# Stick-breaking attention on one core: splitting one k-tile's products in two pieces of columns at eight places

## The reference

```python
h, gate_res = ada_modulate(x, c, norm_g, ada_w, ada_b)
gq, gk, gv, glr, sq, sk, sv, gate = _split(h @ in_w, ODD_SIZES)
...
yd = stick_breaking(hd(sq, SB_HEADS, SB_HEAD_DIM), hd(sk, SB_HEADS, SB_HEAD_DIM),
                    hd(sv, SB_HEADS, SB_HEAD_DIM)).reshape(B_, S, SB_WIDTH)
y = jnp.concatenate([yc, yd], axis=-1) * jax.nn.silu(gate)
return x + gate_res * (y @ out_w)
...
z = jnp.einsum('bthd,bshd->bhts', q[:, q0:q1], k[:, :q1]).astype(jnp.float32) * scale
log_1m = jnp.where(strict, jax.nn.log_sigmoid(-z), 0.0)
after = lax.cumsum(log_1m, axis=3, reverse=True) - log_1m
w = jnp.where(strict, jnp.exp(log_beta + after), 0.0)
outs.append(jnp.einsum('bhts,bshd->bthd', w.astype(v.dtype), v[:, :q1]))
```

## Time and profile before

| what | value |
|---|---|
| time, median of 3 runs | 812.6 us (812.37 to 813.02) |
| profiled execution, its own time | 812.26 us |
| span of that execution, first to last instruction | 810.3 us |
| mean granted TensorE clock | 0.998 of full speed |
| TensorE matmuls | 795.8 us busy (98%), 6984 instructions |
| TensorE weight loads | 784.7 us busy (97%), 6984 instructions |
| VectorE, ScalarE | 641.0 us (79%), 499.2 us (62%) |
| part that the change touches | from 687.06 us to 756.79 us of the span |

### The profile page before, as it was taken

The page is one execution under the profiler, slowest core; times in us unless marked ns, Lnnn a source line. Parts: engine busy times, 40 slices in busy tenths (PEclk is TensorE's granted clock), DMA queues, the critical chain, the costliest instruction groups (busy, mean ns, idle before and its releaser), DMA issues.

```text
span 810.3 us, 17222 instructions
## 1 busy us (share of the span) xinstructions
PE 795.8 (98%) x6984; PEld 784.7 (97%) x6984; DVE 641.0 (79%) x1032; ACT 499.2 (62%) x899; POOL 110.1 (14%) x133
## 2 busy tenths in 40 slices
PE   6999999999999999999999999999999999999996
PEld 6999999999999999999999999999999999999996
DVE  7788599977987879787998899887997568566673
ACT  6576666756667464656676853554686467566652
POOL 0022265401040000000230300001203130000001
PEclk9999999999999999999999999999999999999999
DMA  9934544566567989898777667675665446554441
GB/s 335 392 96 140 179 132 129 154 200 214 193 211 232 366 298 332 310 326 328 254 255 223 219 186 234 227 249 176 207 179 163 138 126 195 180 152 153 148 128 53
DMA packets 47021, 170.41 MB, mean 210 GB/s; under 512 B 5216, under 2 KB 5472, under 8 KB 46688
## 3 DMA queue, kind: packets, MB, share of 16 engines
q1 hardware_dynamic: 46224, 165.31, 61.8%
q10 hardware_dynamic: 720, 4.01, 1.2%
HBM read 168.26 MB, written 1.05 MB: 209 GB/s over the span
## 4 chain that ended last, share of the span: by engine, by line
PE 96%; DVE 1%; ACT 1%; DMA 1%; POOL 1%; issue 0%; SPq 0%; DVEq 0%; POOLq 0%; ACTq 0%
PE bank L196 95%; DMA raw<-in_ws 1%; POOL sq L235 1%; PE bank L199 0%; DVE wl L235 0%; SPq L193 0%; ACT wh L205 0%; ACT sq L202 0%; ACT B1h L202 0%; DVE gd L235 0%; DVE h L223 0%; DVE h L235 0%; DVEq L337 0%; POOLq L337 0%; DVE vt L235 0%
## 5 line engine op out<-in xcount | busy, mean ns | idle before, releaser
L235 DVE TENSOR_TENSOR wl<-raw,wh 128x1024 fp32r<-128x1024 f32 (+1 forms) x260 | 326.2, 1266 | 21.1 <-ACT wh L205 19.9
L205 ACT CAST wh<-raw 128x1024 fp32r<-128x1024 f32 (+1 forms) x260 | 268.9, 1046 | 102.3 <-DMA raw<-in_ws 51.0
L196 PE MATMUL bank<-XAh,wl 128*128 128x256 f32 (+1 forms) x896 | 253.9, 283 | 0.0
L196 PE MATMUL bank<-XAl,wh 128*128 128x256 f32 (+1 forms) x896 | 248.5, 277 | 0.0
L196 PE MATMUL bank<-XAh,wh 128*128 128x256 f32 (+1 forms) x896 | 248.4, 277 | 0.0
L196 PEld LDWEIGHTS bank<-XAh,wl 128*128 128x128 f32 x896 | 168.4, 188 | 2.2 <-issue 0.7
L196 PEld LDWEIGHTS bank<-XAh,wh 128*128 128x128 f32 x896 | 168.5, 188 | 0.1
L196 PEld LDWEIGHTS bank<-XAl,wh 128*128 128x128 f32 x896 | 168.4, 188 | 0.0
L196 PE MATMUL bank<-B1h,wl 128*128 128x256 f32 (+1 forms) x464 | 129.3, 279 | 0.0
L196 PE MATMUL bank<-B1l,wh 128*128 128x256 f32 (+1 forms) x464 | 128.6, 277 | 0.0
L196 PE MATMUL bank<-B1h,wh 128*128 128x256 f32 (+1 forms) x464 | 128.6, 277 | 0.0
(11 more groups left out here) (280 smaller groups left out, 1205.3 us busy)
## 6 DMA issues: line engine op xcount, KB each, us to landing
raw<-in_ws SPq DMA_DIRECT2D x306, 512.0 KB, 4.5
bias<-in_bias ACTq DMA_DIRECT2D x1, 1664.0 KB, 11.8
hK<-in_xk SPq DMA_DIRECT2D x4, 272.0 KB, 5.0
h<-in_xt ACTq DMA_DIRECT2D x1, 1088.0 KB, 7.2
out<-gd SPq DMA_DIRECT2D x4, 256.0 KB, 2.6
raw<-in_ws SPq DMA_DIRECT2D x2, 256.0 KB, 3.7
C<-in_cst SPq DMA_DIRECT2D x1, 512.0 KB, 8.0
crow<-in_crow ACTq DMA_DIRECT2D x1, 512.0 KB, 5.9
```

Of the source, the lines that this page charges most:

```text
L196: return self.real.matmul(*a, **k)
L205: return self.real.copy(*a, **k)
L235: return self.real.tensor_tensor(*a, **k)
```

## The change

In the first unit of each of the eight labels in the table `SPLIT`, one k-tile (the second, k = 1) of the first result tile has its three products made in two pieces of columns. The first piece has the number of columns in the table, 128 or 192, and the second has the rest of the 256. Where tokens move (`sq1`, `sq2`, `sq3`, `oo0`), the new function `in_two` does it, after 6 matmuls of the unit. Where weights move (`sv0` to `sv3`), `three_wide` gets the table's width as its step, after 3 matmuls. Both keep the order of the three products and issue the two pieces of a product one after the other, with the same stationary operand. Everything else stays: data, buffers, semaphores and order.

```diff
+SPLIT = {"sv0": 128, "sq1": 128, "sv1": 192, "sq2": 128, "sv2": 128, "sq3": 192, "sv3": 192, "oo0": 128}
...
                     for c in range(0, width, step):
-                        m = e.matmul(dst[:, c:c + step], a[i], b[j][:, c:c + step], start=first and n == 0 and c == 0,
-                                     stop=last and n == 2 and c + step == width)
+                        z = slice(c, min(c + step, width))
+                        m = e.matmul(dst[:, z], a[i], b[j][:, z], start=first and n == 0 and c == 0,
+                                     stop=last and n == 2 and c + step >= width)
+                return m
+
+            def in_two(dst, a, b, c):
+
+                for i, j in ((1, 0), (0, 0), (0, 1)):
+                    for n in (slice(0, c), slice(c, 256)):
+                        m = e.matmul(dst[:, n], a[i], b[j][:, n], start=False, stop=False)
                 return m
...
+                            if label in SPLIT and (q, k, b, t) == (0, 1, 0, 0):
+                                m = in_two(tile(label, t), (hi[:, k, s], lo[:, k, s]),
+                                           (cols(X[0][:, xk + k, :]), cols(X[1][:, xk + k, :])), SPLIT[label])
+                                continue
...
-                                               512 if label == "vn" and col and q == 6 else 256)
+                                               512 if label == "vn" and col and q == 6 else
+                                               SPLIT[label] if label in SPLIT and (q, k, b) == (0, 1, 0) else 256)
```

## The result

The changed kernel takes 814.82 us (median of 10 runs) against 812.9 us (10 runs) of the kernel before: ratio 1.0025, 95% interval 1.0017 to 1.0033, or +1.92 us. The forecast was 814.45, or +1.85 us.

The account below looks back on a forecast made before the run. TensorE's matmul stream was taken to bound the kernel. Pieces add 2.65 us, the quicker pace behind them gives back 0.80 us: +1.85 us, forecast 814.45 us, range 813.3 to 815.5 us.

Parts of the forecast that it names:

- What bounds the kernel: From 685.98 us TensorE's unbroken 110.26 us chain piece covers all places; changes there go to the end one to one.
- The price of a piece: At the eight places, each piece costs its load, 0.112 us; +0.33 us a place, +2.65 us in all.
- What comes back: Matmuls behind the cuts return from 0.1179 to 0.1135 us each; at most 180 matmuls, -0.80 us.
- I take nearly all: Choice, between 0 and -0.80 us, of how much the quick pace behind the cuts gives back; -0.80 entered the sum.
- 192 with 64 costs what 128 with 128 does: At the cut places, the load sets the price of any piece shorter than 256 columns, whichever way 256 is divided.
- The exception: In `sq1` the scores ran at 695.55, yet the next unit still took 2.91 us; a break is no sure cure.
- the cure: The pieces end the slow pace behind them, giving back up to 0.80 us; missing at half the places or more: 0.22.
- When the dull pace begins: From `sv0` on, the slower pace was said to begin with the matmul at which the moving side changes.
- dull pace: Matmuls of 256 columns start 0.1179 us apart instead of 0.1135, with no other engine waited for.
- the count of ten units: Both units of `sv0` and `sq1`, first units of the other six labels: each 0.09 us too long, 0.9 us in all.

Follow-up runs that it names:

- e3: The changed kernel with `sv1`, `sq3` and `sv3` cut in steps of 64 columns instead of 192 (twelve pieces in `sv1` and `sv3`); 815.62 us.
- e11: The changed kernel with all places cut 128 with 128 and each piece using only 64 of its 128 stationary columns, leaving its result incomplete; 813.21 us.
- e12: The changed kernel with two products cut 128 with 128 and the third 192 with 64 at all eight places; 814.68 us, a single run.
- e9: The changed kernel with each product cut into 64 and then 192 columns at all eight places; 814.47 us.
- e10: The kernel before with one cut only: the first product of the second k-tile in `sq1` in two pieces of 128; 812.46 us.
- e4: The changed kernel with all cuts at 128, each in the second unit of its label instead of the first; 814.85 us.
- e6: The kernel before without cuts; side groups before a change of side, and the scores in `sq1`, moved behind the next unit's first k-tile; 812.27 us.
- e7: As e6, plus one product in `sv0` cut in two pieces; 811.89 us.
- e2: The changed kernel with all eight places cut at 192 with 64 columns; 814.76 us.
- e5: The changed kernel with all places cut at 128, but only the first of the three products in two pieces; 812.89 us.

## Why the prediction was right

**What bounds the kernel** held: the change went to the end one to one, through TensorE's stream. The chain's piece on TensorE stayed unbroken through all eight places, and no other engine came into it there.

**The price of a piece** was the main term, and right: 0.69 us expected for six pieces, 0.68 measured, so +0.325 a place where +0.33 stood. Single places agree: the first matmul of `sq1` comes 0.16 us later behind `sv0` (0.15 expected), and the first unit of `sq2` takes 3.19 us (3.17). The reading that it is the load is shown from both sides: by e3 (pieces half as wide, twice as many, twice the price) and by e11 (stationary operand and load halved, 0.06 instead of 0.11 us). Where the price shows differs from the forecast: the six starts and the first whole one lie within 0.62 us, a little under the 0.64 to 0.71 expected, since the first piece takes only its columns (0.06 us) and the first whole matmul waits for its load instead. The trace agrees with the 0.107 us that the Trainium skill (TensorE: Matmul & The Clock Gate, section "LDWEIGHTS (loading the stationary operand)") gives for 128 columns; the measured distance in a run of short pieces is 0.11. It does not agree with the 0.081 us of that page's "Back-to-back issue gap", which would have given 812.9 us.

**What comes back** was over-sized. "I take nearly all" was 180 matmuls and 0.80 us; it was 129 matmuls and 0.57 us, because behind the three cuts of 192 with 64 the pace stayed dull. The step that failed is the half of the sentence "192 with 64 costs what 128 with 128 does" that I drew without saying it: the price is the same, the effect isn't. The last piece was 64 columns, and e12 and e9 show that at these places this is what matters.

**The exception** that made me doubt the cure, `sq1` behind a dull `sv0`, is not general: it concerns the scores as a break, not a cut of 128 with 128 (e10), and it goes away once `sv0` is quick (e4, e6 with e7). But it is not tied to `sv0` either: in e11 the scores fail in `sq2`, `sq3` and `oo0` as well.

**When the dull pace begins** was read too narrowly. In the last attention it does begin at the change of the moving side. Elsewhere it also begins without one. Timeline of the kernel before from 176 to 184 us, with tokens moving in both units:

```profile
176.48 0.28 PE L196 MATMUL bank<-B0h,wl 128*128 128x256 f32 x1
...
178.88 0.59 PE L196 MATMUL bank<-sq,C 128*128 128x256 f32 x2
179.31 1.03 PE L196 MATMUL bank<-AT,iN 128*128 128x256 f32 x4
...
180.96 0.28 PE L196 MATMUL bank<-B0h,wl 128*128 128x256 f32 x1
...
183.43 0.59 PE L196 MATMUL bank<-sq,C 128*128 128x256 f32 x2
```

The 21 distances up to 178.88 are 0.114 us, the 21 up to 183.43 are 0.118, with only side groups between the two. The two units after that are dull as well, and so are 47 matmuls from 91.57 on, some 115 matmuls or 0.5 us that the count of ten units leaves out. The unit of `oo2` in the changed kernel is such a case too.

**Hits by luck.** The stretch from `sv0` to `oo0` grew by 2.10 us in the trace and the medians by 1.92; the forecast was 1.85. The missing cures (+0.23) stand within the scatter of single executions, so the median can't show that this term was off; the trace does.

**What stays open** is what the dull pace is. It is 0.0044 us or 4% per matmul. Every cut with full-width loads whose last piece was 128 or 192 columns ended it, the only cuts that ended it with a last piece of 64 were those in `sv0` (e2, e12), and no cut with half-wide loads did (e11). Why is not shown. It is not the transfers: in the kernel before, the share of the DMA engines is 0.00 from 697 to 699 us, where the pace is dull, and 0.76 from 684 to 686.9, where it is quick. One trace sign may lead further. In all fourteen traces, look at the scores and weighted values that come in a dull stretch of the last attention with tokens moving before and after them: the group's first matmul takes 0.215 us to its successor in the six cases in which the pace stays dull behind it, and 0.217 to 0.219 in the 32 in which it ends. So whether such a group cures seems settled before it has run, and the dull pace may have more than one form. No run looked into that.

## What to carry to other kernels

Count loads as well as columns: in this stream, with 128 stationary columns, six pieces of 64 to 192 moving float32r columns cost 0.68 us, as much as six whole matmuls of 256 (6 x 0.1135), so a cut costs a whole matmul's time. When a stream runs a few per cent slower behind some point, see what the gain could be at most (here 0.9 us) before paying for a cure, and look first for work that has to be issued anyway and can stand there: moving the side groups cured six places for nothing (e6, 0.38 us by the trace), where the 48 pieces cured five for 2.6 us.

## What was not expected of the hardware

The same matmul, same shape and same granted clock (1.00), has two stable paces, 0.1135 and 0.118 us. Streams as long as the 48 matmuls of `sv0` hold the dull one to the end, and one pair of pieces of 128 columns ends it (e5), but only with full-width loads: with loads of 64 columns (pieces 0.06 us apart) the pace stays at 0.118, with 128 (0.11 us apart) it goes to 0.1135.
